# Three stages of a one-core, three-block network rewritten: forgetting attention as a pipeline over pairs of heads, the setup's loads and order, and ScalarE's order in the gating mixer

## The reference

```python
m = silu(cond) @ w_ada + b_ada                       # (1024, 6144), for c and for c_ctx
h = rmsnorm(x, norm1_w) * (1 + scale) + shift        # then h @ w_in
...
z = gelu(h @ w_in); u, v = split(z, 2)               # gating: v (512, 2048)
v = layernorm(v, ln_g, ln_b)
s = einsum("gts,bnsgc->bntgc", tril(w_s), v) + b_s   # chunks of 128, 8 groups
return (u * s) @ w_out
...
q, k, v, f_logit = split(h @ w_qkvf)                 # forgetting attention, 16 heads of 64
cum = cumsum(log_sigmoid(f_logit + b_f))             # per head, over the tokens
logits = q @ k.T / 8 + cum[q, None] - cum[None, k]   # causal; softmax over k
return (softmax(logits) @ v) @ w_o
```

## Time and profile before

| | us |
|---|---|
| median of 3 runs | 4088.93 (4085.08 to 4095.08) |
| the profiled execution, its own time | 4089.7 |
| its span in the trace | 4088.0 |
| PE busy | 3831.8 (94%) |
| DVE busy | 2172.2 (53%) |
| ACT busy | 1506.1 (37%) |
| POOL busy | 413.8 (10%) |
| granted TensorE clock, mean | 0.969 of full speed |

### The profile page before, as it was taken

One profiled execution on the slowest core, in us unless ns is written; L12 is line 12 of the kernel. 1 busy time (PEld: TensorE's weight loads), 2 busy tenths in 40 slices (PEclk: granted clock), 3 DMA queues, 4 the chain that ended last, 5 costly groups with the idle time before them and its releaser, 6 DMA issues. The chain is left out here.

```text
span 4088.0 us, 48957 instructions
## 1 busy us (share of the span) xinstructions
PE 3831.8 (94%) x18863; PEld 3117.8 (76%) x18863; DVE 2172.2 (53%) x2860; ACT 1506.1 (37%) x2382; POOL 413.8 (10%) x354
## 2 busy tenths in 40 slices
PE   7999888889999999999989989999999999977999
PEld 5788665567878878887778867887988887866887
DVE  4998445547553454436764665344344644355653
ACT  4564434434342332222522223223342323244332
POOL 2672122210000000002131200000000000000000
PEclk9999889989999999999999999999999999988999
DMA  5244522323323333333310023333222333400332
GB/s 169 83 130 129 169 90 90 98 82 95 96 83 97 95 92 98 97 96 96 93 37 0 0 87 99 98 96 93 91 80 80 97 95 92 135 16 10 96 96 87
DMA packets 588884, 364.06 MB, mean 89 GB/s; under 512 B 16647, under 2 KB 570455, under 8 KB 588199
## 3 DMA queue, kind: packets, MB, share of 16 engines
q1 hardware_dynamic: 583136, 349.67, 28.8%
q10 hardware_dynamic: 5575, 11.97, 0.8%
HBM read 345.70 MB, written 15.89 MB: 88 GB/s over the span
## 5 line engine op out<-in xcount | busy, mean ns | idle before, releaser
L1152 PE MATMUL later_bank<-arena 128*128 128x512 f32 (+1 forms) x6792 | 1448.0, 375 | 31.7 <-DVE arena L1125 27.2
L1152 PEld LDWEIGHTS later_bank<-arena 128*128 128x128 f32 x6792 | 1204.1, 190 | 270.9 <-DVE arena L1125 40.1
L1152 PE MATMUL middle_bank<-arena 128*128 128x512 f32 x4944 | 1140.9, 392 | 25.8 <-DVE arena L2604 9.9
L1117 ACT ACTIVATE arena<-arena 128x1024 fp32r<-128x1024 f32 (+2 forms) x526 | 545.3, 1037 | 1591.7 <-PE later_bank L1152 759.7
L1152 PEld LDWEIGHTS middle_bank<-arena 128*128 128x128 f32 x4944 | 928.0, 188 | 241.3 <-DVE arena L1125 27.1
L1125 DVE TENSOR_TENSOR arena<-arena 128x1024 fp32r<-128x1024 f32 (+2 forms) x526 | 639.6, 1216 | 566.7 <-ACT arena L1117 566.0
L1152 PE MATMUL front_bank<-arena 128*128 128x512 f32 (+3 forms) x1776 | 353.6, 360 | 13.9 <-DVE arena L1125 10.3
L1152 PEld LDWEIGHTS front_bank<-arena 128*128 128x128 f32 (+1 forms) x1776 | 296.0, 191 | 67.1 <-DVE arena L1125 12.8
L1300 POOL TENSOR_TENSOR arena<-arena 128x512 f32<-128x512 f32 x120 | 178.2, 1485 | 154.8 <-ACT arena L1505 138.5
L1634 DVE SCALAR_TENSOR_TENSOR arena<-arena,columns 128x512 f32<-128x512 f32 x120 | 131.7, 1153 | 4.3 <-DVE arena L1577 0.8
L1611 DVE SCALAR_TENSOR_TENSOR arena<-front_bank,columns,arena 128x510 f32<-128x510 f32 (+1 forms) x224 | 126.5, 626 | 4.0 <-ACT arena L1441 3.2
(11 more groups left out here) (488 smaller groups left out, 3719.9 us busy)
## 6 DMA issues: line engine op xcount, KB each, us to landing
arena<-in_w_in SPq DMA_DIRECT2D x90, 512.0 KB, 3.8
arena<-in_ffn_w_gate SPq DMA_DIRECT2D x76, 512.0 KB, 3.7
arena<-in_ffn_w_up SPq DMA_DIRECT2D x76, 512.0 KB, 3.7
arena<-in_w_mlp SPq DMA_DIRECT2D x64, 512.0 KB, 3.8
arena<-in_w_ada SPq DMA_DIRECT2D x48, 512.0 KB, 5.4
arena<-in_ffn_w_down SPq DMA_DIRECT2D x48, 512.0 KB, 3.8
ssd_cum_rows<-scratch_cum SPq DMA_DIRECT2D x64, 256.0 KB, 6.1
arena<-in_gm_w_in SPq DMA_DIRECT2D x32, 512.0 KB, 3.8
```

Of the source, the lines that this page charges most:

```text
L1117: act.activation(self.high[q % self.AHEAD][:, 0:kb * cols], self.raw[g % RING][:, 0:kb * cols], ACT.Copy).then_inc(self.high_done, 1)
L1152: ins = pe.matmul(out, still, moving, start=first and n_pass == 0, stop=last and n_pass == 2)
```

## The change

It has three parts; nothing else in the program differs.

**Setup.** Sixteen slots of the arena that are free at that time take the sixteen first steps of `w_ada`, each with a semaphore of its own, so no load waits for the ring. ScalarE's queue keeps only the loads of the first parameter tile (ten); the other 33 go to SyncE's queue, three ahead of each weight step from the third on. TensorE turns one parameter tile, the tokens, does units 0 to 3, turns the scaled tokens, does units 4 and 5, turns the six other parameter tiles, does units 6 and 7. The squares of the context move behind the start of the first gate unit, its transposes from the eight gate units to the units 3, 5, 7, 9, 11, 13, 14 and 15. ScalarE makes the whole scaled tokens of the last four blocks, VectorE those of the first four; the second split comes after the fourth block.

```diff
+    FIRST_SLOTS = (24, 26, 28, 30, 64, 66, 68, 70, 58, 60, 62, 50, 52, 54, 84, 86)
...
+        for n, step in enumerate(self.first_steps):
+            if n == 2:
+                sp.wait_ge(self.zeroed, 1)
+            for tile, row, count, col, ap in islice(later, 3 if n >= 2 else 0):
+                sp.dma_start(self.raw[row:row + count, tile, col:col + ap.shape[1]], ap).then_inc(self.later_params_in, 16)
...
+            sp.dma_start(step, src).then_inc(self.first_landed[n], 16)
...
+        pe.wait_ge(self.params_in, 16 * len(self.first_params))
+        pe.transpose(to_bank()[:, 0:P], self.raw[:, 0, :], core.ident[:]).then_inc(self.turned, 1)
+        pe.wait_ge(self.x_in, 16)
+        turn_tokens()
+        pe.wait_ge(self.cond_ready, 1)
+        for i in range(4):
+            self.first_modulation(pe, i)
+        pe.wait_ge(self.scaled, 4)
+        turn_tokens()
+        for i in range(4, self.FIRST_ADA - 2):
+            self.first_modulation(pe, i)
+        pe.wait_ge(self.later_params_in, 16 * len(self.later_params))
+        for k in range(1, tiles):
             pe.transpose(to_bank()[:, 0:P], self.raw[:, k, :], core.ident[:]).then_inc(self.turned, 1)
```

```diff
-    LAG = 5
+    LAG = 6
...
+        flow.split_high(act, vj.step0 + 2)
         self.into.root_of_tokens(act, rg.banks[7], 1, rg.core.eps2)
...
-                for c in range(CH):
+            if s < 2:
+                for c in (2 * s, 2 * s + 1):
...
-            if s == 2:
+            if s in (3, 4):
                 act.wait_ge(self.var_ready, 1)
-                for c in range(CH):
+                for c in (2 * s - 6, 2 * s - 5):
```

```diff
-    NJ = 2 * CH
+    NJ, BUFS, TURN_AFTER = 2 * CH, 8, 4
...
+        for h in range(FH):
+            pool.tensor_tensor(in_blocks(self.cum_masked[:, h, :]), in_blocks(self.cum_k[:, h, :]),
+                               self.causal.unsqueeze(1).to_broadcast([P, CH, P]), ALU.subtract).then_inc(self.cum_masks, 1)
+        for m in range(DB * NJ):
...
+            pool.wait_ge(self.inverted, m + 1)
+            pool.tensor_scalar(buf, buf, self.rden[:, m % NJ:m % NJ + 1], None, ALU.mult).then_inc(self.normed, 1)
...
+        def stay_busy(count):
+
+            for n in range(count):
+                pe.matmul(pt_banks[0][:, n % 4 * P:(n % 4 + 1) * P], core.ident[:], self.q[:, n % DB, 0:P], start=True, stop=True)
...
+        for j in range(-1, pairs + 3):
+            if j + 1 < pairs:
+                scores(j + 1)
+            if j < 2:
+                stay_busy(8)
+            if 0 <= j - 2 < pairs:
+                turn(j - 2)
+            if 0 <= j - 3:
+                weighted_sums(j - 3)
...
+            if m < last:
...
+                if i:
+                    dve.scalar_tensor_tensor(buf[:, 0:n - P], bank[:, 0:n - P], cum_q, self.cum_k[:, h, 0:n - P], ALU.add, ALU.subtract)
+                else:
+                    dve.wait_ge(self.cum_masks, h + 1)
+                dve.scalar_tensor_tensor(buf[:, n - P:n], bank[:, n - P:n], cum_q, self.cum_masked[:, h, n - P:n],
+                                         ALU.add, ALU.subtract).then_inc(self.s_masked, 1)
+                dve.wait_ge(self.s_masked, m + 1)
+                dve.tensor_reduce(self.top[m % 4], buf[:, 0:n], axis=AX.X, op=ALU.max, negate=True).then_inc(self.top_ready, 1)
+            if 0 <= m - 1 < last:
+                x = (m - 1) % NJ
+                dve.wait_ge(self.exps, m)
+                dve.reciprocal(self.rden[:, x:x + 1], self.den[:, x:x + 1]).then_inc(self.inverted, 1)
...
+                dve.tensor_tensor(self.o_low[:, b, :], o_banks[b % 2][:, :], self.o_high[:, b, :].bitcast(F32), ALU.subtract).then_inc(self.low_done, 1)
```

More of the change, by code:

```diff
@@ L1358, in half, with first_modulation @@
         return self.ada_banks[n % 2][:, 0:256]
+    def first_modulation(self, pe, i):
+        if i >= 2:
+            pe.wait_ge(self.mod_out, i - 1)
+        for part in range(2):
+            pe.wait_ge(self.first_landed[2 * i + part], 16)
+            w = self.first_steps[2 * i + part]
+            for k in range(4):
+                rows = slice(64 * (k % 2), 64 * (k % 2) + 64)
+                ins = pe.matmul(self.half(i)[rows, :], self.cond[:, 4 * part + k, :], w[:, k, :], start=part == 0 and k < 2, stop=part == 1 and k >= 2)
+        ins.then_inc(self.first_done, 1)
+        if i:
+            self.columns(pe, i - 1)
     def modulation(self, pe, i, j):
@@ L1429, in scalar @@
             flow.split_high(act, j.split0 + 2)
+            if j is units[0][2]:
+                act.wait_ge(self.context_in, 16)
+                squares(4, 6)
             if kind == "gate":
@@ L1529, in vector @@
         dve.tensor_reduce(self.sel, core.ident[:].rearrange("p (j c) -> p c j", j=2), axis=AX.X, op=ALU.add).then_inc(self.chosen, 1)
[L1530 to L1533 removed]
+        dve.wait_ge(self.turned, 1)
+        dve.tensor_copy(core.columns[:, 0:P], self.banks[0][:, 0:P]).then_inc(self.taken, 1)
         for k in range(DB):
[L1535 removed]
+            m = 1 + k
             dve.wait_ge(self.turned, m + 1)
@@ L2319, in tensor @@
+        pe.wait_ge(self.s_masked, last)
         flow.multiply(pe, self.outj)
```

364 lines of the change are left out of this document (175 added, 189 removed).

## The result

The changed kernel took 3989.31 us (median of 4 runs, 3983.87 to 3993.24) against 4088.04 for the kernel before in the same session: ratio 0.9754, 95% interval 0.9738 to 0.977, so 98.7 us less, between 94 and 107. Its profiled execution has a span of 3990.6 us. Forecast were 4001, with a range of 3980 to 4040.

What follows compares the result with a forecast made beforehand. TensorE, busy 94% of the span, was taken as the bound, with gains only where it waits or is clocked low. Attention -67, setup -16 and mixer -6 gave -89 from 4089.7: 4001 us, range 3980 to 4040.

Steps and rivals of the forecast that it cites:

- Attention: -67 forecast: Attention: pipelined head pairs remove the waiting, -65 us, and the first out groups about -2 more.
- VectorE's 12.7 us a head pair: Attention loop: VectorE sets the pace at 12.7 us for each of eight head pairs.
- the 12 to 14: Attention, sign of being right: 12 to 14 us between the first maxima of two head pairs, VectorE busy over 90%.
- the out product's start: Attention, sign of being right: the out product begins 105 to 112 us after the first scores.
- my 6.5: Attention: filling and draining the pipeline takes 6.5 us on top of the eight head pairs.
- TensorE's share, 9.0 to 11.2 us a pair: Attention: TensorE's scores, transposes and weighted sums at full clock take 9.0 to 11.2 us a pair, under VectorE's cover.
- The rival that TensorE stays at the lower level: Attention: TensorE's clock stays low, 17 us a pair, +34 us, 4035 in all; chance 0.12.
- The chain between engines: Attention: VectorE's reciprocal waits for ScalarE's exponential, 14.5 us a pair, +14 us, 4015 in all; chance 0.12.
- The slow loads: Setup: first loads run at 240 GB/s, so it gains only 6 to 10 us, 4009 in all; chance 0.08.
- Setup: -16 forecast: Setup: first dense matmul at 41.3 instead of 58.26 us, -17, with small give-backs; -16, between -10 and -19.
- The waits for a split near 100 to 170 us: After the setup, sign of being wrong: new waits for a split near 100 to 170 us.
- Mixer: -6 forecast: Gating mixer: divided squares -6.5 us, an earlier split about -1, longer lag +1.7; -6, between 0 and -9.

Runs made afterwards that it cites:

- part alone: The kernel before with only the attention part of the change applied; 4007.52 us, ratio 0.9801 to the kernel before.
- GpSimd's second pass: The changed kernel with a second GpSimd pass, times 1.0, over each block of probabilities; 4042.80 us, ratio 0.9883.
- fox_recip_of_pairs: The changed kernel with one reciprocal of two columns for both heads of a pair step instead of two of one; 3993.66 us, ratio 0.9763.
- fox_mask_added: The changed kernel with logits from one scalar_tensor_tensor over all columns and the causal mask added by VectorE, as before; 4001.31 us, ratio 0.9782.
- gating_lag5: The changed kernel with the mixer's gates five steps behind again instead of six; 3985.98 us, ratio 0.9746.

## Why the prediction held, and where its terms were off

**Attention: -67 forecast, -81 measured (part alone, timed), -82 by the spans of the traces.** The mechanism was right: VectorE at over 90%, everything else under its cover, shown by the mask and by GpSimd's second pass. The term that was mis-sized is VectorE's 12.7 us a head pair; it measured 10.37, which is even below the 10.6 that I had as the lower bound, and outside the 12 to 14 that I had named as the sign of being right. (The other sign that failed is the out product's start, 93.0 us behind the first scores instead of 105 to 112.) Three things are in it. I charged 35 ns between dependent instructions on top of full durations. A maximum does start 34 ns behind the scalar_tensor_tensor that it needs. But the other neighbours don't need each other's results, and where nothing is waited for the second starts 83 ns before the end of the first. The durations of a pair add up to 11.4 us, the overlaps and gaps take 1.4 off and the waits put 0.4 on. And the reciprocal of one column takes 156 ns, where I took the 204 of eight columns. The row to use for a pipelined sequence is the distance from start to start, not the duration. Filling and draining cost 93.0 - 83.1 = 9.9 us against my 6.5. So 8 x 12.7 + 6.5 = 108 became 93. The two errors had different signs, and the first (18.5 us) was over five times the second (3.4): that the forecast of the whole came within 10 us owes something to that.

One reading of the old loop was the wrong way round. The prediction has the clock fall after VectorE's wait at the pair's end. In the trace it falls inside that wait (from 3626.8 to 3631.8), and TensorE's last turns and weighted sums, which VectorE waits for, run at half the clock:

```profile
3628.00:3632.00 4.00, 4.00 (x20) 4.00 (x20) 0.20 (x1) 0.67 (x2) 0.00 (x0) 0.50 0.00 0
```

So the 4.8 us were in part the low clock's. Both are gone, and the sum didn't need them apart.

Smaller terms: the -38 at 16 us a pair leaves out the 2 us that the -84 has. GpSimd's 7.8 us a pair were 68.5 / 8 = 8.6, since 128 columns take it 0.60 us and not a quarter of the 1.56 for 512. The scores were counted as eight instructions of 531 ns, at most 4.2 us, but L2278 has 128 records, sixteen in a pair, so 4.2 was no upper bound by that row. They took 26.6 / 8 = 3.3, because the two heads' start 7 ns apart.

**TensorE's share, 9.0 to 11.2 us a pair, came out at 71.64 / 8 = 9.0,** with the drains of the mode changes in it. They can be read now, where each kind of product is followed by one of another mode (L2348 64 rows, L2358 full, L2369 64 columns):

```profile
3600.63 0.92 PE L2348 MATMUL later_bank<-arena 64*128 64x384 f32 x4
...
3601.47 1.09 PE L2358 MATMUL later_bank<-ident,arena 128*128 128x128 f32 x8
...
3602.49 0.88 PE L2369 MATMUL later_bank<-arena 128*64 128x128 f32 x12
```

Each group begins 0.07 to 0.08 us before the end of the last matmul of the one ahead. Inside the group of turns the trace has them 0.109 us apart, each 0.27 long, and the next group starts 0.20 after the last of them: 0.09 us lost, 1.1 us for the twelve changes of a pair, where the prediction had 3.7 as the other end. The rule of the Trainium skill, "TensorEngine Tiling (Array Packing)", section "Key Properties", that a change of mode drains the array, agrees in kind with these rows; its price here is a third of a matmul's duration. No run took the changes out, so this is a reading of the rows and not an experiment.

**The clock.** The rival that TensorE stays at the lower level failed: 0.98 in the loop, though a third of its busy time are transposes (27.6 of 79.6 us in the stage). A single fall costs 1.5 us, as the loops of 83.1 and 81.6 us show; in the run with the mask, at 0.87 for the stage, VectorE covered it. The statement of the Trainium skill, "TensorE: Matmul & The Clock Gate", section "Part 4: PE-mode transpose", on which part of that rival stood, changed nothing here; whether a loop of transposes alone would keep the clock, no run shows.

**The other rivals.** The chain between engines cost 0.4 us of the 10.37 in this form (waits of 0.24 and 0.17), but it was nearer than its chance of 0.12 said: half a pair step of delay (`fox_recip_of_pairs`) made it the pace. The slow loads: the setup's gain at the first dense matmul was 16.6, so they kept up. GpSimd: 1.56 us for 512 columns, as in the earlier trace rows, in the middle of a full loop.

**Setup: -16 forecast, 12.7 timed, 13.3 in means of traces.** The working by stages was within a microsecond (41.3 against 42.24). What was too small is what is given back, 3.3 us where I had 1 net. I had put it into the stretch around 110 us, where VectorE is busy 9.85 of 10. There the lead is still 17.9 us; it is lost between the 91st and the 97th product, near 270 us, in a wait for a split behind a VectorE that is just as full (9.87 of 10 from 265 to 275), with the lower clock behind it. That the moved pieces are the cause was tried and not confirmed. The waits for a split near 100 to 170 us, which I had named as a sign of being wrong, are there (2.6, 3.2 and 2.8 us in the changed kernel), but the kernel before has three of 2.3 to 2.6 too.

**Mixer: -6 forecast, 5.7 timed, 7.4 in the traces.** The stall and the clock behind it were 6.9 us by experiment against 6.5 worked out; the sixth step of lag cost 2.6 against 1.7, since the whole gate of 2.78 us is on the path and not only what TensorE has less. The rest of the gain, 3.1 us, is there by 2905 us, where only the places of the splits are new; I had put it at 1. The wait of 4.25 us of the earlier trace rows is 1.40 there, and the clock from 2875 to 2892 us is 1.00, where it was 0.83 from 2884 to 2904; all three traces with the old mixer have a fall there and none of the new. 3.1 + 6.9 - 2.6 is the 7.4. That the forecast came so near the timed value is partly two terms too small that offset each other.

## What to carry to other kernels

Cost a pipelined loop by the engine with the most work in it, in distances from start to start, and then ask of the second thing: the round trip through all engines has to fit into the steps between issue and use, and when it doesn't, taking work from the busiest engine makes the loop longer. What such a cut can save is the distance between two starts too, not the duration of what goes. A block of ScalarE or VectorE work that can wait belongs behind the next weight split, in pieces. And one trace is one sample: before explaining a give-back of 7 us between two traces, look at the same stretch in traces where nothing in it was changed.

## What the runs showed that I had not expected

Stages that no kernel changed differ from trace to trace by 3 to 4 us, and in two of them it is the granted clock, not work. At the entry of the merge of the second block's branches (near 2380 us) and in the scan of the first block (near 855 us) TensorE is sparse, and when the clock falls depends on the run. The changed kernel, at the first place and at the second:

```profile
2375.00:2385.00 10.00, 6.45 (x25) 2.76 (x24) 5.04 (x10) 4.49 (x9) 0.10 (x1) 0.83 0.56 185
2385.00:2395.00 10.00, 9.38 (x31) 6.89 (x32) 5.60 (x7) 4.92 (x8) 0.00 (x0) 0.83 0.91 366
850.00:860.00 10.00, 7.13 (x25) 5.33 (x24) 4.89 (x12) 0.01 (x1) 0.00 (x0) 0.68 0.00 0
860.00:870.00 10.00, 10.00 (x63) 9.43 (x63) 4.51 (x9) 0.00 (x0) 0.00 (x0) 0.80 0.00 0
```

`fox_mask_added` at the first place, and `gating_lag5` at the second, with the same instructions:

```profile
2374.00:2384.00 10.00, 5.84 (x29) 2.90 (x29) 6.60 (x12) 4.64 (x9) 0.10 (x1) 1.00 0.58 189
2384.00:2394.00 10.00, 10.00 (x39) 6.97 (x38) 7.06 (x8) 5.19 (x8) 0.00 (x0) 1.00 0.96 380
```
```profile
849.00:859.00 10.00, 7.13 (x45) 5.95 (x44) 6.16 (x15) 0.00 (x0) 0.00 (x0) 1.00 0.00 0
859.00:869.00 10.00, 10.00 (x63) 7.94 (x63) 6.39 (x11) 0.00 (x0) 0.00 (x0) 1.00 0.00 0
```

Between the landmarks around them, the first place takes 3.1 us less at the full clock and the second 4.3. In `gating_lag5` the scan has its fall all the same, only later (0.54 from 876 to 887 us), where TensorE is busy 4.0 us of 11. A change upstream moves such a stretch by some microseconds, and whether that alters the odds of a fall there these runs don't settle; it bounds what one profile can say about a change worth less than about 5 us.
